# Differential attention's input projection with eleven of twelve steps as seven quarter-size products

## What is computed

```
def diff_attention(x, w_qkv, w_o, lam, subln_g, lambda_init):
    B, S, _ = x.shape
    q, k, v = jnp.split(x @ w_qkv, 3, axis=-1)
    ...
```

## Time and profile before

| | us |
|---|---|
| median of 3 runs | 3141.19 |
| lowest, highest | 3140.52, 3145.33 |
| span of the profiled execution | 3142.1 |
| TensorE busy in it | 2835.0 |
| VectorE busy in it | 1428.3 |
| the projection's stage, first to last matmul start | 1384.48 to 1515.24 |

### The profile page before, as it was taken

One profiled execution on the slowest core, in us unless ns is written; L12 is line 12 of the kernel. 1 busy time (PEld: TensorE's weight loads), 2 busy tenths in 40 slices (PEclk: granted clock), 3 DMA queues, 4 the chain that ended last, 5 costly groups with the idle time before them and its releaser, 6 DMA issues. The chain is left out here.

```text
span 3142.1 us, 64907 instructions
## 1 busy us (share of the span) xinstructions
PE 2835.0 (90%) x27341; PEld 2091.7 (67%) x27341; DVE 1428.3 (45%) x2504; ACT 902.1 (29%) x1584; POOL 325.8 (10%) x462
## 2 busy tenths in 40 slices
PE   7999999999999999999888996965889999996985
PEld 5866778887667888888665663643567876763652
DVE  5678578632774433222654221214695654221222
ACT  2256432222573222122642000004433342000002
POOL 2125211001500000000000000002022330000001
PEclk9999999999999999999999998986999999998997
DMA  9730267542324233422129999995123128999997
GB/s 288 205 81 2 55 200 235 154 113 75 81 59 108 78 97 86 124 74 92 74 98 407 380 425 427 425 426 201 49 67 85 42 67 336 426 424 427 425 425 290
DMA packets 380047, 638.92 MB, mean 203 GB/s; under 512 B 92668, under 2 KB 329889, under 8 KB 345769
## 3 DMA queue, kind: packets, MB, share of 16 engines
q1 hardware_dynamic: 341497, 560.04, 48.8%
q0 software_dynamic: 17056, 51.63, 4.6%
q10 hardware_dynamic: 21264, 23.88, 2.2%
HBM read 611.06 MB, written 24.38 MB: 202 GB/s over the span
## 5 line engine op out<-in xcount | busy, mean ns | idle before, releaser
L2728 DVE TENSOR_TENSOR moe_scratch<-masks_b,moe_ps 128x128 f32<-128x128 f32 x102 | 39.5, 388 | 636.8 <-ACT masks_b L2585 636.8
L2527 PE MATMUL moe_ps<-moe_ring,moe_scratch 128*32 128x256 f32 x3616 | 234.4, 410 | 83.8 <-DMA moe_ring<-in_moe_w_gu 74.7
L527 PE MATMUL chain_ps<-ffn_xhi,ffn_whi 128*128 128x512 f32 x704 | 274.3, 390 | 2.5 <-DVE ffn_xlo L750 1.6
L528 PE MATMUL chain_ps<-ffn_xlo,ffn_whi 128*128 128x512 f32 x704 | 273.9, 389 | 0.0
L529 PE MATMUL chain_ps<-ffn_xhi,ffn_wlo 128*128 128x512 f32 x704 | 273.9, 389 | 0.0
L2527 PEld LDWEIGHTS moe_ps<-moe_ring,moe_scratch 128*32 128x32 f32 x3616 | 141.1, 116 | 168.6 <-issue 87.8
L2512 PE MATMUL moe_ps<-xT,causal 128*32 128x256 f32 x3296 | 205.7, 387 | 0.0
L2585 ACT ACTIVATE masks_b<-moe_ps 128x128 f32<-128x128 f32 x102 | 28.3, 277 | 495.2 <-PE moe_ps L2527 493.3
L2512 PEld LDWEIGHTS moe_ps<-xT,causal 128*32 128x32 f32 x3296 | 127.8, 113 | 58.9 <-issue 10.0
L527 PEld LDWEIGHTS chain_ps<-ffn_xhi,ffn_whi 128*128 128x128 f32 x704 | 132.2, 188 | 31.4 <-issue 2.6
L529 PEld LDWEIGHTS chain_ps<-ffn_xhi,ffn_wlo 128*128 128x128 f32 x704 | 132.2, 188 | 27.3
(11 more groups left out here) (804 smaller groups left out, 6083.9 us busy)
## 6 DMA issues: line engine op xcount, KB each, us to landing
moe_ring<-in_moe_w_gu SPq DMA_DIRECT2D x80, 2048.0 KB, 37.4
moe_ring<-in_moe_w_down SPq DMA_DIRECT2D x40, 2048.0 KB, 34.6
da_moe_units<-in_moe_w_gu SPq DMA_DIRECT2D x24, 2048.0 KB, 37.9
rw_AR<-in_moe_w_gu SPq DMA_DIRECT2D x24, 2048.0 KB, 40.4
ffn_came<-in_ffn_w_in SPq DMA_DIRECT2D x88, 512.0 KB, 5.2
da_moe_units<-in_moe_w_down SPq DMA_DIRECT2D x12, 2048.0 KB, 32.2
rw_AR<-in_moe_w_down SPq DMA_DIRECT2D x12, 2048.0 KB, 29.4
ffn_out_w<-in_ffn_w_out SPq DMA_DIRECT2D x16, 1408.0 KB, 7.0
```

What stands on the lines that cost most here:

```text
L527: nc.tensor.matmul(out, high, self.xhi[k], start=(k == 0), stop=False)
L528: nc.tensor.matmul(out, high, self.xlo[k], start=False, stop=False)
L2527: last = nc.tensor.matmul(psGU[j * BLK:(j + 1) * BLK].rearrange("p (g a n) -> p g a n", g=2, a=2), xbT[:, k], cols[:, j], start=(k == 0), ...
L2728: V.tensor_tensor(h.rearrange("p (a m i) -> p a i m", a=2, m=2), gated.rearrange("p (a i m) -> p a i m", a=2, m=2), psU.rearrange("p (a i ...
```

## The change

Step 0 stays as it was. Each of the steps 1 to 11 becomes seven products of quarters, in the manner of Strassen and Winograd. The weights of a step (1024 inputs x 256 outputs) are cut in four blocks `A11`, `A12`, `A21`, `A22`: by output tile (first digit) and by even or odd input tile (second digit). x is cut in `B11` ... `B22` by even or odd input tile and by the first or second 256 tokens. A plain block product needs eight block products; this form needs seven, each of 4 input tiles, 128 outputs and 256 tokens, and with three split products for each: 7 x 4 x 3 = 84 matmuls of 128 x 128 weights against 256 columns.

In return there are sums. Of x, once: `T1` = B12 - B11, `T2` = B22 - T1, `T4` = B21 - T2, `T3` = B12 - B22, all on VectorE, and each is split in high (ScalarE) and low (VectorE) again. Of the weights, in each of the 11 steps, on GpSimd: `S1` = A21 + A22, `S2` = S1 - A11, `S4` = A12 - S2, `S3` = A21 - A11 (`sum_weights`). Seven blocks of 128 x 512 are then split (A11, A12, A22, S1, S2, S4, S3), ScalarE writing the high and VectorE the low part. They lie in 13 slots, each for a high and a low block; a slot is free again when the product that read it is done. The seven products land in seven half banks of PSUM, ScalarE copies the first one to SBUF (`copy_first`), and VectorE makes the four quarters of the result by seven additions of 128 x 256 (`join`), each with one operand in SBUF and one in PSUM, the last two by the way of partial sums. The result goes to `projT`. The scale of 1/8, which ScalarE applied on the way out, is now applied when the weights are split (in steps 1 to 3).

Also, `ChainNorm` (a norm that the chain uses elsewhere) keeps three semaphores instead of seven, with the waits counted higher; nothing is moved there. Outside the stage, every engine's order of instructions is the same as before.

The core of the diff:

```
+class Winograd(Dense):
...
+    HALF = SEQ // 2
+    PRODUCTS = ("A11", "S4", "S1", "S2", "S3", "A12", "A22")
+    PREPARED = ("A11", "A12", "A22", "S1", "S2", "S4", "S3")
...
+    def slot(self, i, what):
+        return (7 * (i - 1) + self.PREPARED.index(what)) % len(self.hi_slots)
+
+    def wait_for_slot(self, eng, i, what):
+        was = 7 * (i - 1) + self.PREPARED.index(what) - len(self.hi_slots)
+        if was >= 0:
+            eng.wait_ge(self.product_done, was // 7 * 7 + self.PRODUCTS.index(self.PREPARED[was % 7]) + 1)
+        elif self.slot(i, what) >= self.early_slots:
+                eng.wait_ge(self.products_done, 1)
...
+        if i == 2:
+            sp.wait_ge(self.low_done, self.split_at(0))
+        else:
+            sp.wait_ge(self.weights_low, 7 * (i - 3) + 3)
+            sp.wait_ge(self.summed, 4 * (i - 2))
...
+    def sum_weights(self, pool):
+        tt, ALU = self.B.nc.gpsimd.tensor_tensor, self.B.ALU
+        for i in range(1, self.n):
+            self.wait_loaded(pool, i)
+            block = lambda what: self.block_of_weights(i, what)
+            into = lambda what: self.sum_slots[self.slot(i, what)]
+            self.wait_for_slot(pool, i, "S1")
+            tt(into("S1"), block("A21"), block("A22"), ALU.add).then_inc(self.summed, 1)
+            self.wait_for_slot(pool, i, "S2")
+            pool.wait_ge(self.summed, 4 * (i - 1) + 1)
+            tt(into("S2"), into("S1"), block("A11"), ALU.subtract).then_inc(self.summed, 1)
+            self.wait_for_slot(pool, i, "S4")
+            pool.wait_ge(self.summed, 4 * (i - 1) + 2)
+            tt(into("S4"), block("A12"), into("S2"), ALU.subtract).then_inc(self.summed, 1)
+            self.wait_for_slot(pool, i, "S3")
+            tt(into("S3"), block("A21"), block("A11"), ALU.subtract).then_inc(self.summed, 1)
...
+    def seven(self, pe, i):
+        mm = self.B.nc.tensor.matmul
+        for p, (what, of_x, out) in enumerate(zip(self.PRODUCTS, ("B11", "B22", "T1", "T2", "T3", "B21", "T4"), self.regions)):
+            pe.wait_ge(self.weights_low, 7 * (i - 1) + self.PREPARED.index(what) + 1)
+            if i == 1 and of_x[0] == "T":
+                pe.wait_ge(self.x_sums_low, {"T1": 1, "T2": 2, "T3": 2 + self.places_of_t3, "T4": 3 + self.places_of_t3}[of_x])
+            if i == 1 and what == "A22":
+                pe.wait_ge(self.act_done, 1)
+            if i >= 2:
+                if what == "A11":
+                    pe.wait_ge(self.copied, i - 1)
+                else:
+                    pe.wait_ge(self.joined, 7 * (i - 2) + {"S4": 3, "S1": 3, "S2": 3, "S3": 5, "A12": 6, "A22": 7}[what])
+            s = self.slot(i, what)
+            pairs = self.kt // 2
+            for j in range(pairs):
+                xhi, xlo = self.moving(of_x, j)
+                mm(out, self.hi_slots[s][:, j], xhi, start=(j == 0), stop=False)
+                mm(out, self.hi_slots[s][:, j], xlo, start=False, stop=False)
+                last = mm(out, self.lo_slots[s][:, j], xhi, start=False, stop=(j == pairs - 1))
+            last.then_inc(self.product_done, 1)
...
+    def scalar(self, act, before, after):
+        for k in range(1, self.kt):
+            self.x_high(act, k)
+        for what in ("A11", "A12", "A22"):
+            self.weight_high(act, 1, what)
+        self.x_sum_high(act, "T1")
+        self.weight_high(act, 1, "S1")
+        self.x_sum_high(act, "T2")
+        self.weight_high(act, 1, "S2")
+        self.weight_high(act, 1, "S4")
+        self.take_on_act(act, 0)
+        self.x_sum_high(act, "T3")
+        self.weight_high(act, 1, "S3")
+        self.x_sum_high(act, "T4")
+        for i in range(1, self.n):
+            if i + 1 < self.n:
+                for what in self.PREPARED[:3]:
+                    self.weight_high(act, i + 1, what)
+            self.copy_first(act, i)
+            if i + 1 < self.n:
+                for what in self.PREPARED[3:]:
+                    self.weight_high(act, i + 1, what)
...
+    def vector(self, dve, before, after):
+        tt, ALU = self.B.nc.vector.tensor_tensor, self.B.ALU
+        for k in range(1, self.kt):
+            self.x_low(dve, k)
+        for what in ("T1", "T2", "T4"):
+            self.sum_x(dve, what)
+        for what in ("A11", "A12", "A22"):
+            self.weight_low(dve, 1, what)
+        self.x_sum_low(dve, "T1")
+        self.weight_low(dve, 1, "S1")
+        self.x_sum_low(dve, "T2")
+        self.weight_low(dve, 1, "S2")
+        self.weight_low(dve, 1, "S4")
+        self.sum_x(dve, "T3")
+        self.x_sum_low(dve, "T3")
+        self.weight_low(dve, 1, "S3")
+        self.x_sum_low(dve, "T4")
+        v, t, w = self.partial
+        a, d, c, b, e, f, g = self.regions
+        for i in range(1, self.n):
+            first = self.first_copy[i % 2]
+
+            def join(out, one, other):
+                tt(out, one, other, ALU.add).then_inc(self.joined, 1)
+            made = lambda count: dve.wait_ge(self.joined, 7 * (i - 1) + count)
+            done = lambda count: dve.wait_ge(self.product_done, 7 * (i - 1) + count)
+            if i + 1 < self.n:
+                for what in self.PREPARED[:6]:
+                    self.weight_low(dve, i + 1, what)
+            dve.wait_ge(self.copied, i)
+            done(4)
+            join(v, first, b)
+            made(1)
+            join(t, v, c)
+            made(2)
+            join(self.places(i, 0, 1), t, d)
+            done(5)
+            join(self.places(i, 1, 1), t, e)
+            join(w, v, e)
+            if i + 1 < self.n:
+                self.weight_low(dve, i + 1, "S3")
+            done(6)
+            join(self.places(i, 0, 0), first, f)
+            done(7)
+            made(5)
+            join(self.places(i, 1, 0), w, g)
...
-    last = Dense(B, "da_in", 12, 2, KD, qkv_loads(B), [x0[:, 0]] + tiles_of(xhi, KD - 1), [x0[:, 1]] + tiles_of(xlo, KD - 1), (w0[:], w1[:]), (high0[:], high1[:]),
...
+    FREE, SLOT = 162820, 2 * PAIRS * P * 4
+    slot_places = [FREE + q * SLOT for q in range(9)] + [NEXT_LOW + SLOT] + [FREE + q * SLOT for q in range(12, 15)]
...
+    last.pool_body = last.sum_weights
```

More of the change, by code:

```diff
@@ new lines, in attention_input @@
+    x0_sum, x_sum = at("x0_sum", [P, 2, SEQ], NEXT_X), at("x_sum", [P, KD - 1, SEQ], 93188)
+    beside = lambda T: T[:, 1::2, HALF:]
+    whole = lambda name, high, low: [(slice(0, PAIRS), block(name + "_hi", high), block(name + "_lo", low), block(name, low, F32))]
+    sums_of_x = {"T1": whole("t1", BASE, BASE + SLOT), "T2": whole("t2", FREE + 10 * SLOT, FREE + 11 * SLOT), "T4": whole("t4", NEXT_LOW, FREE + 9 * SLOT),
+                 "T3": [(slice(0, 1), x0[:, 0:1, HALF:], x0[:, 1:2, HALF:], x0_sum[:, 1:2, HALF:]), (slice(1, PAIRS), beside(xhi), beside(xlo), beside(x_sum))]}
@@ L1971, in attention_input @@
+    last.set_up("da_in", 9, hi_slots, lo_slots, sum_slots, sums_of_x, regions, (small[:, 0], small[:, 1]), (small[:, 2], partial[:], last_partial[:]),
+                lambda i: HD ** -0.5 if i < 4 else 1.0, lambda i, o, c: projT[:, 2 * i + o, c * HALF:(c + 1) * HALF])
+    last.pool_body = last.sum_weights
     return projT, last
```

136 lines of the change are left out of this document (116 added, 20 removed).

## The result

The changed kernel takes 3148.13 us (median of 10 runs, 3143.43 to 3152.13) against 3140.56 us before on the same chip (10 runs, 3139.3 to 3145.33): ratio 1.002, 95% interval 1.0012 to 1.0028, so 3.8 to 8.8 us slower. So the 3142.1 us of before, which is a span too, lies some 2.7 us above the median of its device times in like terms, and not 0.9; the forecast of 5.0 us more does not hang on it.

What follows compares the result with a forecast made beforehand. TensorE's matmuls were taken to bound the stage. Waits of 8.9 and 3.8 us, then 99.4 us for 69 products, put the attention at 1522.0 against 1516.99, 5.0 us later: 3146.2 us, range 3137 to 3155.

Steps and rivals of the forecast that it cites:

- Slower by over 0.2%: Whole kernel: a time over 3147.5 us, given a chance of 0.37.
- TensorE's share: Steps 1 to 11: 924 matmuls of 256 columns at 0.120 us take 110.9 us, a gain of 8.7.
- 0.113: Rival for the matmul's price: the extra 0.013 us grows with the columns; 5.8 us less, 3140 to 3143; chance 0.25.
- the last 69 products: From step 2's second product on: 69 x 12 matmuls at 0.120 us take 99.4 us.
- The turns: Step 1: eight GpSimd additions cost VectorE 1.07 us each, 8.6 in all; TensorE idles 8.9 us for S4.
- four additions for step 3 fall in it: VectorE's work ahead of step 2's second product: four GpSimd additions fall within it and cost 4.3 us.
- it waits 3.8 us more: Step 2's second product: TensorE, there at 1417.7, waits until 1421.5, 3.8 us more.
- the clock might fall after the first wait: After step 1's 8.9 us idle: half pace loses about 2.6 us, hidden because TensorE waits until 1421.5 anyway.
- The later steps: Steps 3 to 11: TensorE counted as last at 10.1 us a step, VectorE about even at 9.3 to 10.3.
- the rival in which VectorE bounds each step: All four additions meet low parts, 11.4 us a step: 3158 us, chance 0.13.
- The rest of the program keeps its order.: After the stage: what the change does to the attention's start, 5.0 us later, it does to the kernel.
- the rivals named above: Wkv stage, rival in 5 and 6: new semaphores or places in SBUF slow the copy; no chance given.

Runs made afterwards that it cites:

- experiment 2: Changed kernel with each of GpSimd's additions on one element, so the result is not the projection: stage 126.9 us against 135.9; total 3129.04 us, not comparable.
- experiment 4: Changed kernel, GpSimd beginning step 2's sums only when step 1's S4 low part is done: 3150.59 us, ratio to before 1.0017 to 1.0037.
- 1: Changed kernel with all sums of weights on VectorE and GpSimd idle: 3141.07 us, ratio to before 0.9993 to 1.001.
- Experiment 8: Changed kernel with 34 unread matmuls of 512 columns between the first two products of step 1: 3150.6 us, ratio to before 1.0021 to 1.0048.
- Experiment 10: Changed kernel with 34 unread 512-column matmuls in step 1's wait, GpSimd starting step 3's sums after six low parts of step 2: 3150.17 us.
- 6: Changed kernel with 144 satisfied waits put into TensorE's program in the wkv stage, moving later code: 3147.85 us, ratio to before 1.0014 to 1.0032.
- 7: Changed kernel with weight sums of steps 1 and 2 on VectorE, GpSimd's from step 3, and 144 satisfied waits in the wkv stage: 3145.2 us.
- 12: Changed kernel with all weight sums on VectorE and the g_w1 load issued behind the next two chunks' loads: 3140.13 us, ratio to before 0.9983 to 1.0002.
- 9: Changed kernel with all weight sums on VectorE and 34 unread matmuls of 128 columns in step 1's wait: 3143.17 us, ratio to before 0.9994 to 1.0012.
- 11: Changed kernel with 34 unread matmuls of 128 columns behind the first product of step 1: 3149.71 us, ratio to before 1.0014 to 1.0033.
- 3: Kernel before the change with 23 more unread matmuls at the end of the stage: 3144.42 us, ratio to before 0.9998 to 1.0016.
- 5: Kernel before the change with 104 satisfied waits in TensorE's program in the wkv stage, moving later code: 3141.32 us, ratio 0.9992 to 1.001.

## Why the prediction was right, and where it was not

3146.2 was predicted and 3148.1 measured; against before that is 5.0 us more predicted and 7.6 measured. Slower by over 0.2% had 0.37: by the medians the result is 0.24% slower, by the ratio of the runs it lies on that bound. That the two totals are so near is in part luck: the stage grew by 1.6 us less than forecast, and the total by some 4 us more than the stage, of which the prediction had nothing.

- **TensorE's share.** 0.120 us a matmul, as taken from the extra of 0.013 that does not shrink with the columns; 0.113 and 0.109 are out. The term is large enough to turn the sign of the stage: at 0.113 the last 69 products would be 5.8 us shorter, more than the 3.4 that it grew by (an estimate from the prediction's own sum). So are the turns: without them the stage is 5.6 us shorter than before (experiment 2).
- **The turns.** S4's low part was predicted 23.1 us after the stage's start and the product came after 23.16; the wait was to be 8.9 us and is 8.94. A turn of 1.07 us is 1.06 in experiment 4, and with all eight gone (2) S4 comes 8.4 us earlier, 1.05 a turn. The page SBUF — State Buffer of the Trainium skill ("SBUF: two separate sides") has VectorE instructions with two SBUF inputs and GpSimd's hold the port by turns; the trace agrees, and 1 and 2, which take away GpSimd's half of it, show that it costs 6 to 9 us here.
- **The step that failed: "four additions for step 3 fall in it", and so "it waits 3.8 us more".** Two fell in it, and there was no second wait. I had noted that the clock might fall after the first wait and called it hidden; but it held TensorE back by 2.0 us (4.65 us from 1407.14 to 1411.79, where one interval of 0.22, as behind the short wait at 1396.51, and 20 of 0.120 are 2.62), and with it the product ends that free GpSimd's slots. GpSimd's sums came late enough to miss two of the four turns. Experiment 8, with the clock kept up, has just the four turns and the 3.82 us that were predicted. In this order of work the slow clock and the second wait exclude each other; I had them side by side. (In 4, where step 2's own sums were held back, both occur.) VectorE is through with step 1's third join at 1419.0 and TensorE comes to step 2's second product at 1419.4, so the wait was missed by a narrow margin. From S4 to the attention this makes -3.8 + 2.0, and the stage became 3.4 us longer instead of 5.0.
- **The later steps.** TensorE is the bound in all of them, 10.1 us a step; the rival in which VectorE bounds each step is out. Experiment 10 shows how near it is.
- **"The rest of the program keeps its order."** It does, but not its time. The nine other kernels with the change whose totals compare, and the changed one itself, are 0.8 to 4.2 us slower than their stages explain, 2.9 in the mean; the two variants of before are 2.0 faster and 0.6 slower. The profiles show 2 to 3 us more in the wkv products (133.2 to 134.3 us in all but 8, 129.8 to 131.0 in the kernels before), as a later load, a wait and a fall of the clock; in 6 and 7 it is the 144 waits that hold them up. In the changed kernel, 1, 2, 4 and 12 a fetch of code began 1.79 to 1.97 us into the copy, and the copy took 5.4 to 5.5 us; in all others none began within it, and it took 3.8 to 4.3. That explains the late load there, but not in 9 to 11, where the wait was still 1.2 to 1.7 us. The new semaphores and the new places in SBUF, the rivals named above, were not tested by themselves. That stays open, and with intervals of 5 us on the medians the 2.9 is a mean over kernels, not shown for one.

So of the +7.6 us in the medians the stage accounts for 3.4; the 2.8 us more in the wkv products may account for as much again, which one profile of each kernel does not show. Profile against profile the span grew by only 2.4 us: -0.5 ahead of the stage, +3.4 in it, -4.6 from there to the wkv products (893.5 us in this profile of before, 888.9 and 889.5 in 3 and 5, 888.9 in the changed kernel), +2.8 in them and +1.3 behind. A stretch that the change doesn't touch can thus differ by over 4 us between single executions.

## What to carry to other kernels

Before work is given to an idle GpSimd, look at what VectorE does at that time: where both have their operands in SBUF alone, each addition of 128 x 512 cost VectorE 1.07 us, more than the 0.60 for which VectorE would have done it itself. Where three engines release each other, a delay of one moves the collisions of the other two; a wait or a slow clock can't be priced without asking which releases it delays, and filling a wait can make the stage longer. Seven products for eight could pay, with no turns, 5.6 us of the 15 that the columns promise: 6 of the 15 are lost since each matmul had 0.013 us of its own, the rest in the wait of 1.90 us and the low clock behind it.
